# A gated retention block with 32 experts on eight cores: the prefix state as a pipeline, weights relaid in 8 KB runs, casts spread over the main tiles

## The reference

```
h = modulate(rms_norm(x, gain1), shift1, scale1)
a, q, k, v, rg, ga, gb = split(h @ w_in)            # 2048 -> 9216 columns
q, k = rotary(q, positions), rotary(k, positions) * 128**-0.5
y_pool = pool_mixer(a, w_pool) @ w_branch_pool      # causal means of 2, 4, 8, 16
y_ret = retention(q, k, v, rg) @ w_branch_ret       # 8 heads, chunks of 128, a decayed state
x = x + gate1 * ((sigmoid(ga) * y_pool + sigmoid(gb) * y_ret) @ w_out)
h2 = modulate(rms_norm(x, gain2), shift2, scale2)
x = x + gate2 * moe(h2)     # 32 experts in 4 groups, top 2; (silu(h2@w1) * (h2@w3)) @ w2
out = rms_norm(x, final_gain)
```

## Time and profile before

| | us |
|---|---|
| median of 3 runs | 18169.23 (18060.0 to 18257.98) |
| the profiled execution's own time | 18305.63 |
| its span, core 3, the slowest | 18304.1 |
| shortest span, core 0 | 17553.9 |

### The profile page before, as it was taken

How to read it: one execution, slowest core, us unless ns; L and a number is a source line. 1 busy time by engine, 2 the same in 40 slices (tenths; PEclk the granted TensorE clock), 3 DMA queues, 4 the chain that set the end, 5 groups by cost and what they waited for, 6 DMA issues and landing times. The chain is left out here.

```text
span 18304.1 us, 163529 instructions; the slowest of 8 cores (17553.9 to 18304.1 us)
## 1 busy us (share of the span) xinstructions
PE 9345.2 (51%) x52713; PEld 5913.8 (32%) x52713; DVE 3369.9 (18%) x9731; ACT 2940.6 (16%) x5915; POOL 2406.7 (13%) x2870
## 2 busy tenths in 40 slices
PE   7233333665454355434553455435443558877773
PEld 6111111222243344323442344324332423333331
DVE  0112222333211111111111111111111112212222
ACT  0011111333211110111111111111111111111112
POOL 0011111111100000000000000000000023323331
PEclk8566666777666667666766676667665667777886
DMA  7644444334466556665666556655765486787735
GB/s 204 143 82 86 91 86 95 76 79 83 73 144 140 116 133 143 137 123 131 145 142 126 119 140 146 134 115 141 142 141 114 117 285 214 239 287 247 240 96 176
DMA packets 2151676, 2595.42 MB, mean 142 GB/s; under 512 B 109431, under 2 KB 2031664, under 8 KB 2050736
## 3 DMA queue, kind: packets, MB, share of 16 engines
q0 software_dynamic: 254752, 1208.87, 31.9%
q1 hardware_dynamic: 1891472, 1342.53, 26.4%
q10 hardware_dynamic: 4608, 33.56, 0.4%
HBM read 3405.88 MB, written 643.83 MB: 221 GB/s over the span
## 5 line engine op out<-in xcount | busy, mean ns | idle before, releaser
L1115 PE MATMUL p_pf<-p_w,p_xT 128*128 128x512 bf16 x6080 | 1511.4, 415 | 32.3 <-DMA p_w<-w_b,p_idx 15.3
L444 PE MATMUL p_ptr<-ident_b_sb,p_xnb 128*128 128x128 bf16 x2048 | 238.7, 309 | 2236.5 <-DVE p_xnb L440 2236.5
L855 PE MATMUL p_pf<-p_wslot,p_mgT 128*128 128x256 bf16 x4096 | 728.3, 362 | 1107.0 <-DMA p_wslot<-w_out_g 1077.7
L632 PE MATMUL p_pf<-p_wkv,p_hT 128*128 128x512 bf16 x3072 | 897.0, 464 | 755.8 <-DVE p_hT L457 755.8
L884 PE MATMUL p_pf<-p_hT,p_wslot 128*128 128x256 bf16 x8192 | 1207.6, 312 | 32.6 <-DMA p_wslot<-w_in_b 31.2
L1131 PE MATMUL p_py<-p_w,p_hidT 128*128 128x512 bf16 x3040 | 958.3, 485 | 468.6 <-DVE p_yt L1133 395.3
L762 PE MATMUL p_pf<-p_wslot,p_hT 128*128 128x256 bf16 x2048 | 295.9, 318 | 1704.2 <-DMA p_wslot<-w_in_b 1578.6
L884 PEld LDWEIGHTS p_pf<-p_hT,p_wslot 128*128 128x128 bf16 x8192 | 912.3, 112 | 254.5 <-issue 44.8
L855 PEld LDWEIGHTS p_pf<-p_wslot,p_mgT 128*128 128x128 bf16 x4096 | 518.8, 129 | 1316.8 <-issue 1140.5
L444 PEld LDWEIGHTS p_ptr<-ident_b_sb,p_xnb 128*128 128x128 bf16 x2048 | 208.3, 143 | 2256.6 <-issue 2256.6
L1115 PEld LDWEIGHTS p_pf<-p_w,p_xT 128*128 128x128 bf16 x6080 | 632.3, 105 | 865.2 <-issue 599.6
(11 more groups left out here) (233 smaller groups left out, 11747.6 us busy)
## 6 DMA issues: line engine op xcount, KB each, us to landing
p_wslot<-w_in_b SPq DMA_DIRECT2D x576, 1024.0 KB, 8.4
w_b<-w POOLq DMA_DIRECT2D x128, 2048.0 KB
w_b<-w POOLq DMA_DIRECT2D x128, 1024.0 KB
p_wslot<-w_out_g SPq DMA_DIRECT2D x128, 1024.0 KB, 6.4
p_wada<-w_ada SPq DMA_DIRECT2D x48, 2048.0 KB, 12.3
p_x<-x_pre SPq DMA_DIRECT2D x96, 1024.0 KB, 8.0
p_wslot<-w_bp_b SPq DMA_DIRECT2D x64, 1024.0 KB, 6.6
p_wslot<-w_br_b SPq DMA_DIRECT2D x64, 1024.0 KB, 5.8
```

The source lines that it names most:

```text
L632: o("pe", (lambda j, kc, pk: lambda e: e.matmul(out=pk[:, :], lhsT=hT[:, kc, :], rhs=wkv[:, kc, j * 512:(j + 1) * 512], start=(kc == 0), s ...
L855: o("pe", (lambda kc, pt, wv, lc: lambda e: e.matmul(out=pt[:, 0:256], lhsT=mgT[:, kc, lc * 128:(lc + 1) * 128], rhs=wv[:, kc, :], start=( ...
L1115: o("pe", (lambda wu, pp, kc: lambda e: e.matmul(out=pp[:, :], lhsT=xT[:, kc, :], rhs=wu[:, kc, :], start=(kc == 0), stop=(kc == KC - 1))) ...
```

## The change

- Prefix stage: `norm_transpose` is cut into `norm_ssq`, `norm_scale`, `transposes` and the evacuation. `pre_chunk` gives way to a loop that works on four chunks at once: between the projection groups of chunk p stand the transposes of p + 1, the square sum and scaling of p + 2, the x load of p + 5 and the state update of p - 1. x, xnb and the small tiles are tripled, the state's PSUM pair is its own, and the projections have four PSUM buffers.
- `trig_group` computes cosine and sine for 8 chunks at once, with 11 VectorE instructions of up to 512 elements and two Sin, two steps per chunk, one group ahead.
- `T.sub(i)` gives a tile one buffer for each piece: hT and xT are tracked for each of the 16 pieces, the state for each head. `evac_mod` gives ScalarE the pieces of the first PSUM tile and VectorE those of the second, so that the two write and read nothing in common. This holds in all three stages.
- w_in, w_bp, w_br (already on the host) and w_out_g lie in blocks of 128 rows of 4096 elements, so that each `wload` reads 8 KB runs, and the prefix weights arrive in 12 cast loads of 16 KB rows, in tiles of their own. The 44 blocks of w_in and the branches are cast DRAM to DRAM, one every second chunk. w_out_g is stored in phase0 in 512 byte runs.
- No expert cast is issued in the prefix stage. All 256 are issued by `wload`, one at every third load, on POOL.

```
+    def norm_ssq(self, xt, junk, small):
...
+    def norm_scale(self, xt, small, xnb):
...
     def evac_mod(self, ptrs, dst, col0, geff, shift):
-        for kc in range(KC):
-            pt = ptrs[kc // 8]
...
-            if kc % 2 == 0:
...
-                        reads=[pt, geff, shift], writes=[dst])
+        for q8 in range(8):
+            for hb in range(2):
+                kc = hb * 8 + q8
+                pt = ptrs[hb]
...
+                if hb == 0:
...
+                            reads=[pt, geff, shift], writes=[dst.sub(kc)])
...
+            jobs = [("w_in", g) for g in range(36)] + [("w_bp", g) for g in range(4)] + [("w_br", g) for g in range(4)]
+            every = max(1, NP_ // len(jobs))
...
            for p in range(NP_):
+                if p % every == 0 and jobs:
+                    cast_job(*jobs.pop(0))
+                if p % G == 0:
+                    pending = trig_ops(p // G + 1)
+                vb = vbs[p % 2]
+                pk = proj(p, wkv[0])
+                feature_major(p + 1)
+                rot(p, 0, pk)
+                ssq(p + 2)
+                pk = proj(p, wkv[1])
+                rot(p, 1, pk)
+                scale(p + 2)
+                pv = proj(p, wkv[2])
+                vcopy(p, 0, pv, vb)
+                if p > 0:
+                    update(p - 1)
+                pv = proj(p, wkv[3])
+                vcopy(p, 1, pv, vb)
+                kdecay(p)
+                for _ in range(2):
+                    if pending:
+                        pending.pop(0)()
...
             def wload(q, src_ap, k, reads=()):
...
                 self.load(q, slot, view, src_ap, reads=reads)
+                self.nload += 1
+                if self.nload % 3 == 0:
+                    self.cast_weights(1)
...
-            per_tile = -(-len(self.cast_jobs) // (NM // TCH))
...
             def tile_body(ti, a_prev):
-                self.cast_weights(per_tile)
...
-                        slot, wv = wload("sp", d["w_in_b"][:, off + u * 256:off + (u + 1) * 256].rearrange("(k p) n -> p k n", p=128), KC, reads=[self.dbuf["w_in_b"]])
+                        slot, wv = wload("sp", self.w_in_part(off + u * 256), KC, reads=[self.dbuf["w_in_b"]])
```

More of the change, by code:

```diff
@@ L261, in __init__, with sub @@
         self.b = Buf(name)
+        self.subs = {}
+    def sub(self, i):
+        if i not in self.subs:
+            self.subs[i] = Buf("%s_%s" % (self.b.name, i))
+        return self.subs[i]
     def __getitem__(self, k):
@@ L406, in build @@
                 self.a_prev0 = sbm("a_prev0", [128, 1024], BF16)
-                self.op("dve", lambda e: e.memset(self.state[:, :, :], 0.0), writes=[self.state])
+                self.op("dve", lambda e: e.memset(self.state[:, :, :], 0.0), writes=[self.state.sub(h) for h in range(H)])
                 self.phase1()
@@ new lines, in phase1 @@
+            for p in range(3):
+                load_x(p)
+            o("dve", lambda e: e.tensor_copy(out=pos_f[:, :], in_=pos_i[:, :]), reads=[pos_i], writes=[pos_f])
+            wkv = [sb("wkv%d" % j, [128, 2, KC, 256], BF16) for j in range(4)]
+            wa = [sb("wa%d" % j, [128, 2, KC, 256], BF16) for j in range(2)]
+            for w, off in ((wkv, OFF_K), (wa, OFF_A)):
+                for j, t in enumerate(w):
+                    for hh in range(2):
+                        g = off // 256 + j * 2 + hh
+                        self.load("pool", t, t[:, hh, :, :].rearrange("p k n -> p (k n)"), d["w_in"][g * 128:(g + 1) * 128, :])
@@ L605, in conv_w_b @@
-            def conv_w_b(nm, j):
-                cv = cvr.next()
-                cvv = cv[:, :, :].rearrange("p k n -> p (k n)").rearrange("p (k n) -> p k n", k=8)
-                self.load("pool", cv, cvv, d[nm][:, j * 512:(j + 1) * 512].rearrange("(k p) n -> p k n", p=128))
-                self.store("sp", cv, d[nm + "_b"][:, j * 512:(j + 1) * 512].rearrange("(k p) n -> p k n", p=128), cvv, writes=[self.dbuf[nm + "_b"]])
-            for j in range(IN_W // 256):
-                jobs.append((conv_w_in, (j,)))
@@ new lines, in feature_major, with proj @@
+            def feature_major(p):
+                if p < NP_:
+                    self.transposes(xnbs[p % 3], ptrs)
+                    self.evac_mod(ptrs, hTs[p % 2], 0, self.g1eff, self.shift1)
+            def proj(p, w):
+                pt = pkv.next(); hT = hTs[p % 2]
+                for kc in range(KC):
+                    o("pe", (lambda kc: lambda e: e.matmul(out=pt[:, :].rearrange("p (t n) -> p t n", t=2), lhsT=hT[:, kc, :], rhs=w[:, :, kc, :], start=(kc == 0), stop=(kc == KC - 1)))(kc),
+                      reads=[hT.sub(kc), w], writes=[pt])
+                return pt
@@ new lines, in rot, with vcopy, kdecay @@
+            def rot(p, j, pt):
+                cos_t, sin_t = trig[(p // G) % 2]
+                self.rotary(pt, 4, cos_t[:, p % G, :], sin_t[:, p % G, :], [cos_t, sin_t], tring, krots[p % 2], j * 512)
+            def vcopy(p, j, pt, vb):
+                o("act", lambda e: e.activation(out=vb[:, j * 512:(j + 1) * 512], in_=pt[:, :], func=AF.Copy, scale=flags[:, p:p + 1]),
+                  reads=[pt, flags], writes=[vb])
+            def kdecay(p):
+                krot, kd = krots[p % 2], kds[p % 2]
@@ L654, in phase1, with update, trig_ops @@
-            for p in range(NP_):
-                pre_chunk(p)
+            def update(p):
+                self.state_update(kds[p % 2], vbs[p % 2], pst)
+            def trig_ops(g):
+                if g * G >= NP_:
+                    return []
+                cos_t, sin_t = trig[g % 2]
+                return self.trig_group(pos_f, g * G, min(G, NP_ - g * G), tw, cos_t, sin_t)
+            for fn in trig_ops(0):
+                fn()
+            pending = []
+            ssq(0); scale(0); ssq(1); scale(1)
@@ L656, in phase1 @@
+            while jobs:
+                cast_job(*jobs.pop(0))
+            update(NP_ - 1)
+            for j in range(2):
+                pa = proj(NP_ - 1, wa[j])
+                o("act", (lambda j, pa: lambda e: e.activation(out=self.a_prev0[:, j * 512:(j + 1) * 512], in_=pa[:, :], func=AF.Copy))(j, pa),
+                  reads=[pa], writes=[self.a_prev0])
             self.P.emit()
@@ L691, in phase2 @@
             o("dve", lambda e: e.tensor_copy(out=pos_f[:, :], in_=pos_i[:, :]), reads=[pos_i], writes=[pos_f])
-            o("pool", lambda e: e.tensor_copy(out=self.state_bf[:, :, :], in_=self.state[:, :, :]), reads=[self.state], writes=[self.state_bf])
+            o("pool", lambda e: e.tensor_copy(out=self.state_bf[:, :, :], in_=self.state[:, :, :]), reads=[self.state.sub(h) for h in range(H)], writes=[self.state_bf])
             msum = sb("msum", [128, NE], BF16)
```

209 lines of the change are left out of this document (109 added, 100 removed).

## The result

The changed kernel takes 15912.54 us (median, 15734.68 to 16062.86) against 18211.93 us for the kernel before in the same comparison: 2299 us less. Some executions of either kernel have one die at a lower granted clock throughout and take longer; the ratio, 0.8718 with a 95% interval of 0.854 to 0.8897, leaves them out, as do the ratios further down, while the medians include them. The forecast was 14930 us, with a range of 14250 to 15800. The direction was right; the time lies above the range.

The account below looks back on a forecast made before the run. No engine was full: prefix hand-offs, weight-slot waits at main tile starts and expert evacuation held TensorE. 18305.6 - 2365 - 55 - 560 - 280 = 15046 us profiled, 14930 as a median; range 14250 to 15800.

Parts of the forecast that it names:

- Prefix, -2365: Prefix stage: TensorE becomes the bound at 18.9 us a chunk, so the stage takes 1893 us for 4258.
- The rival of the open pipeline: Prefix stage: some hand-off holds a chunk at 28 us, +865, for 15790 us; chance 0.1.
- The clock: Prefix stage: dense cores bring the slower TensorE rate, 18.9 us a chunk against 15.9, worth 285 us.
- Start of the main stage, -55: Main stage start: SP's last constant load stands behind five casts in place of ten, 55 us less.
- Main tiles, -560: Main stage: net 35 us less per tile, times 16; ends -1010 and +150.
- Sum 55 to 127. I take 83: Main tiles: stalls added per tile by casts beside weight loads, 55 to 127 us, taken as 83.
- its own sign of being wrong: Main tiles: the prediction is wrong if tiles stay at 596 us or more.
- What was "gone", 118 of 596: Main tiles: 118 us saved per tile, from the start hole (105), two evacuations (8) and w_out loads (5).
- The burst at the tile start: Main tile start: 5.3 casts leave at once, a load lands per 31 us, TensorE stalls 8 to 33 us.
- Runs of 8 KB: Main tiles: 8 KB runs save 5 us per tile on the seven exposed w_out loads.
- Expert stage, -280: Expert stage: the hole before the third down step goes; half taken between ends 0 and -575 us.
- DMA-bound tiles: Main stage: DMA bounds the tiles at 617 us for 596, 15820 us as a median; chance 0.2.

Follow-up runs that it names:

- with the burst: Changed kernel with all 16 casts of a main tile issued at once at its start: 16488.18 us.
- e1: Changed kernel with all 256 expert casts issued in the prefix loop and none in the main tiles: 15978.82 us.
- e7: e2 with w_out's weight loads issued two ahead, in front of the x1 stores: 14968.87 us.
- e9: e2 with w_out's weights issued two loads ahead and its x pieces one step ahead: 14128.65 us.
- e3: Changed kernel with the old row layout of the bf16 scratch weights, in runs of 512 bytes (branches 1 KB): 16308.44 us.
- e2: Changed kernel with one expert cast per prefix chunk and the rest at every fifth weight load, 10 per main tile: 15203.59 us.

## Why the prediction was wrong, step by step

- **Prefix, -2365: right.** Forecast 18.9 us a chunk; measured 1791 / 96 = 18.7 on core 3. TensorE is the bound, no engine or hand-off holds it. With the start of the main stage the two terms were -2420; the main stage began 2537 us earlier. Of the 117 more, 28 come from phase0, which ended at 664 for 692 in this execution. The rival of the open pipeline is out.
- **The clock: half right.** Half of the cores ran at 1.00 and half at 0.81 to 0.85, with TensorE equally dense on all. The rule that I weighed (the Trainium skill, TensorE: Matmul & The Clock Gate, section Seeing it yourself: once three cores of a die are dense, the die goes to 13/16) gave the right chunk for core 3, but not for the die it is on: this case's rows decide against that part. The time is set by the slow pair, so the sum did not suffer. That core 3, for which it was worked out, was in one is luck: with the burst it ran at 1.00 and its prefix took 1539.
- **Start of the main stage, -55: right.** From the last projection to the first matmul of `a` it is 2614.4 - 2481.5 = 133 us, where the same measure of before is 5151 - 4932 = 219: -86.
- **Main tiles, -560: wrong, +133. This is the step that failed**, and in it the term "Sum 55 to 127. I take 83", the price of the casts. The tile took 604, past the 596 that the prediction had named as its own sign of being wrong. What was "gone", 118 of 596, left 478 for a tile without casts; e1 shows 451, so that side was right, and cautious. The 16 casts cost 153, above the upper end, and the six new ones alone 72. I priced a cast at the DMA time that did not fit beside a stage's loads and let the rest hide. What failed is that overlap, not the DMA time, which was even shorter than forecast: 26.9% x 9672 / 397.81 = 6.5 us per MB for 8.5, or 10.2 per cast. The tile paid 9.6 per cast, with the DMA engines idle 39% of the stage. The likely reason is that a load has only the lead that three slots give, and at w_out none at all; e7 and e9 show it for w_out, and no run had more slots, so elsewhere it is argued. The lower clock on cores 0 to 3 (0.65 for 0.74) needs no term of its own: cores 4 to 7, at 0.69 to 0.70, had tiles as long.
- **The burst at the tile start: right.** Six casts where 5.3 were forecast, 25.1 us for a load to land for 31, 29 us of hole where 8 to 33 were forecast, none over 38.2.
- **Runs of 8 KB: undersized.** 5 us a tile on w_out forecast; 19 on w_out and 37 in all, by e3.
- **Expert stage, -280: wrong.** -58 on core 3, whose expert stage was longer here than in any other version with the new evacuation; undoing the evacuation costs 79 on average, and the shortest of core 3's, 3151 in e7, is 215 below the 3366 of before. The reason given for the lower end (where DMA is the bound nothing comes back) pointed the right way, and half was too much to take: the x gather took over, 896.0 us in e9 for 283.9 before.
- **Which rival was nearest?** DMA-bound tiles, 617 us and 15820, came close to 604 and 15912.54. Its mechanism was not what happened: the DMA share is 0.61, not full; the loads come late one by one.
- **Two slips of arithmetic**, neither of which bears on the outcome. The change loses from 765 us a tile on by the sum's own terms (596 + (18305.6 - 15606) / 16), not from 790. And the casts counted part by part, 5.3 + 2.7 + 2.7 + 4 + 2.7, are 17.4 a tile, as in the first 14 tiles, not 16.

Of the 983 us between forecast and result (15912.54 - 14930), the main tiles are 693 in the profile and the expert stage 222, the better prefix takes back 117, and the rest is the step to a median: the profiled execution lay 0.75% above it before, and 0.4% below it now.

## What to carry to other kernels

Price background transfers near their full DMA time against the stage they run in, if its loads have little lead; here it was 9.6 of 10.2 us. A lead longer than such a transfer takes to land (16.7 to 27.5 us here) might hide them, which no run tested. An idle share of the DMA engines does not show that they hide. Before moving such work, look where it was free: the faster prefix stage still took 96 casts for 4 to 7 us each, against 12 in the main tiles. And read the order of each queue for loads behind a store that waits for a result: a wait that was there without any cast (9.1 us, 112 times) was worth more, 1075 us in e9, than the best placement of the casts, 709 in e2. Last, compare tiles of two versions at equal granted clock, core by core.

## What the runs showed of the hardware that was not expected

- **The lower clock comes by pairs of cores.** From 900 to 2100 in the prefix stage all eight cores keep TensorE busy all the time. In the changed kernel cores 2, 3, 6 and 7 were granted 0.81 to 0.85, the others 1.00. With the old layout it was cores 2 and 3 alone (0.83), with the burst of 16 cores 0 and 1 alone (0.82). In none of these three was a whole die slowed in that stretch. What chose the pairs is not known. Core 3 with the burst, to set beside its row at 0.85 above:

```profile
900.00:2100.00 1200.00, 1200.00 (x6967) 601.95 (x6966) 701.32 (x2173) 545.97 (x1064) 465.40 (x436) 1.00 0.38 105
```

- **A cast's DMA time depends on its company.** POOL's queue took 6.5 us per MB written beside the main stage's loads, and 8.8 where casts filled the engines (89.0% of 3900 us for 396.44 MB, e1 from 900 to 4800). A cast takes 27.5 us (2 MB) or 16.7 (1 MB) to land, by the profile page of the changed kernel:

```profile
w_b<-w POOLq DMA_DIRECT2D x128, 2048.0 KB, 27.5
w_b<-w POOLq DMA_DIRECT2D x128, 1024.0 KB, 16.7
```
